# Weight slots split and released in halves of the contraction

## The chip, the core and the metric

The kernel runs on one core of one Trainium2 chip. The metric is the time of one execution on the device in microseconds (us). Five engines with queues of their own take part: PE (TensorE, matmuls; PEld is its weight load), DVE (VectorE), ACT (ScalarE), POOL (GpSimd), and SP, which here issues the transfers of weights. They wait for each other through semaphores only, and each takes its instructions in the order of its program.

## The reference, cut to what matters

Two transformer-like blocks over 256 tokens of width 1024 in fp32. The first block has two layers that also carry a context stream of 256 tokens. All matrix products have the form below; norms, modulation and attention stand between them.

```python
def adaln_in(x, g, shift, scale):
    return rmsnorm(x, g) * (1 + scale) + shift

def adaln_out(x, y, g, gate, weight):
    return x + weight * gate * rmsnorm(y, g)

def swiglu(h, w_gu, w_down):
    gu = h @ w_gu
    return (jax.nn.silu(gu[..., :D_FF]) * gu[..., D_FF:]) @ w_down

def ffn_sublayer(x, mod, k, g_pre, g_post, w_gu, w_down):
    h = adaln_in(x, g_pre, mod[k], mod[k + 1])
    return adaln_out(x, swiglu(h, w_gu, w_down), g_post, mod[k + 2], HALF_STEP)
...
        merged = (jax.nn.sigmoid(gate_a[:, :s]) * (y_nsa @ w_up_nsa[i])
                  + jax.nn.sigmoid(gate_b[:, :s]) * (y_moba @ w_up_moba[i]))
        x = x + merged @ w_out[i]
```

## The kernel before, in words

All weights pass in 305 **units** (`weight_units`), at most 128 x 2048 numbers (1 MB): 8 chunks of the contraction (k) by 256 output columns for gate-up, projections and mixers, 10 or 12 chunks by 128 columns for the down projections (dn..a and dn..b). A unit is used for the 256 tokens of x (X), the 256 of the context (Z), or all 512. Some gate-up phases are split in ax (tokens of X) and az (of Z), some down phases in bx and bz, so that the norms of one stream run beside matmuls of the other.

Products are made in two parts: w = w_hi + w_lo and h = h_hi + h_lo, and for each k three matmuls are issued, (w_hi, h_hi), (w_hi, h_lo), (w_lo, h_hi) (`PARTS`). So each unit goes through four engines, with two slots (u % 2) of w_raw, w_hi and w_lo:

- SP (`sync_program`, L386): waits until w_lo of unit u-2 is made in both halves, then loads w_raw of unit u.
- ACT (`high_split`, L1260): waits for the transfer and for PE's end with unit u-2 (unit_done), and copies w_raw to w_hi in two halves of the slot.
- DVE (`low_split`, L802): subtracts, w_lo = w_raw - w_hi, in the same halves. These are the halves of the contraction, since k is the outer index of the slot.
- PE (`feature_unit`, L454; `token_unit`; `up_phase`): waits for both halves of w_lo and for the evacuation of unit u-2, and runs all its matmuls: for each 128 output columns m, all k.

ACT and DVE follow an order written out by hand: `turn_of(u)` evacuates unit u from PSUM, splits unit u+2, and finishes u's result (for gate-up: hid and its low part). In a `window`, each turn is followed by `beside(code)`, a few steps of a norm: "v" and "V" are a root (rows named tok), "0" to "3" add a pair of chunks of the residual and square it, "a" to "d" make a pair of chunks of h and its low part. POOL adds the squares (ssum). PE runs the sums over partitions (L436) and the spread of the root (L443) at fixed places between a unit's matmuls (`norms_at`). In some gate-up units DVE also makes the modulation vectors (`mod_products`, L784). `attention` runs between phases; the weights of two units are ready before it.

## Time and profile before

| | before |
|---|---|
| median of 3 runs | 2483.17 us (2473.91 to 2485.79) |
| the profiled execution | 2485.29 us |
| its span | 2483.6 us |
| PE busy | 2318.9 us (93%), 14514 matmuls |
| DVE busy | 1470.1 us (59%) |
| ACT busy | 1030.4 us (41%) |
| POOL busy | 121.1 us (5%) |
| mean granted TensorE clock | 0.933 |
| w_lo halves on DVE | 610, 659.1 us |
| w_hi halves on ACT | 610, 556.9 us |
| a 1 MB weight transfer, issue to landing | 4.8 us median |
| HBM traffic | 151 GB/s over the span |

The span runs from the first to the last instruction. A granted clock of 1.00 is 2.4 GHz, 0.50 is 1.2 GHz; a value between them is the mean over a stretch at the two levels. Matmuls overlap, so PE's busy time is not its rate; the count of matmuls in a stretch over its length is. "[2.05 <-DVE w_lo L807]" behind an instruction is the idle time of its engine just before it, and what ended it.

### The profile page before, as it was taken

What the parts mean: (1) busy time and instruction counts of PE and PEld (TensorE: products, weight loads), DVE (VectorE), ACT (ScalarE), POOL (GpSimd) and SP (SyncE); (2) the same over time, 40 slices, a digit from 0 to 9 for tenths busy, and PEclk for the clock granted to TensorE, in tenths of its full rate; (3) what the DMA queues carried; (4) which work ended last, traced back from release to release, by engine and by line L of the source; (5) the groups of instructions that cost most, each with busy time, mean ns of one, the idle gap of its engine ahead of it and who ended that gap; (6) DMA issues with size and microseconds to landing.
All of it is one profiled execution on the core that took longest, in us unless ns stands there. A gap on an engine that the chain in (4) does not pass through costs nothing. (4 is left out here: it accounts for less than half of the span.)

```text
span 2483.6 us, 35308 instructions
## 1 busy us (share of the span) xinstructions
PE 2318.9 (93%) x14514; PEld 2026.6 (82%) x14514; DVE 1470.1 (59%) x2453; ACT 1030.4 (41%) x1729; POOL 121.1 (5%) x83
## 2 busy tenths in 40 slices
PE   5999998999899999899999988969997999999998
PEld 2988888898798888889888886569997875588998
DVE  5675775667566677565677565635554544345555
ACT  3422224643652223563222354544444544334443
POOL 1000001100200000100000020010000010000000
PEclk8999999999999999999999998979998995589999
DMA  6545554455345555445555442015555420024553
GB/s 255 196 158 200 187 166 156 138 202 169 119 170 168 199 179 171 149 147 174 185 190 178 157 166 89 1 51 172 202 178 195 153 87 16 1 102 147 181 175 127
DMA packets 70362, 376.08 MB, mean 151 GB/s; under 512 B 7454, under 2 KB 12190, under 8 KB 43834
## 3 DMA queue, kind: packets, MB, share of 16 engines
q1 hardware_dynamic: 67536, 367.81, 43.5%
q10 hardware_dynamic: 2666, 6.02, 0.7%
q8 instruction: 115, 1.88, 0.3%
q14 instruction: 45, 0.37, 0.0%
HBM read 372.75 MB, written 1.05 MB: 151 GB/s over the span
## 5 line engine op out<-in xcount | busy, mean ns | idle before, releaser
L467 PE MATMUL ps_g<-h,w_hi 128*128 128x256 f32 (+1 forms) x4224 | 999.3, 331 | 19.1 <-DVE h L874 10.3
L807 DVE TENSOR_TENSOR w_lo<-w_raw,w_hi 128x1024 fp32r<-128x1024 f32 (+2 forms) x610 | 659.1, 1122 | 321.8 <-ACT w_hi L1267 321.4
L467 PEld LDWEIGHTS ps_g<-h,w_hi 128*128 128x128 f32 x4224 | 719.0, 192 | 99.1 <-DVE w_lo L807 11.2
L467 PE MATMUL ps_g<-h,w_lo 128*128 128x256 f32 (+1 forms) x2112 | 695.7, 329 | 0.0
L1267 ACT ACTIVATE w_hi<-w_raw 128x1024 fp32r<-128x1024 f32 (+2 forms) x610 | 556.9, 963 | 204.1 <-PE ps_g L467 180.2
L467 PE MATMUL ps_g<-hid,w_hi 128*128 128x256 f32 (+1 forms) x2368 | 501.2, 310 | 18.9 <-DVE w_lo L807 15.3
L467 PEld LDWEIGHTS ps_g<-h,w_lo 128*128 128x128 f32 x2112 | 405.2, 192 | 36.8
L467 PEld LDWEIGHTS ps_g<-hid,w_hi 128*128 128x128 f32 x2368 | 389.0, 193 | 44.4 <-DVE w_lo L807 17.4
L467 PE MATMUL ps_g<-hid,w_lo 128*128 128x256 f32 (+1 forms) x1184 | 364.6, 308 | 0.0
L1366 ACT ACTIVATE gate_tmp<-ps_g 128x256 f32<-128x256 f32 (+1 forms) x144 | 65.2, 453 | 628.8 <-PE ps_g L467 628.8
L467 PE MATMUL ps_g<-b_h,w_hi 128*128 128x256 f32 x1504 | 282.6, 291 | 10.5 <-DVE b_h L874 7.3
L467 PEld LDWEIGHTS ps_g<-b_h,w_hi 128*128 128x128 f32 x1504 | 240.3, 196 | 14.4 <-issue 9.6
L911 DVE TENSOR_TENSOR prod<-gate_tmp,ps_g 128x256 f32<-128x256 f32 (+1 forms) x128 | 66.6, 521 | 302.3 <-ACT gate_tmp L1366 302.3
L467 PEld LDWEIGHTS ps_g<-hid,w_lo 128*128 128x128 f32 x1184 | 228.3, 193 | 11.0
L467 PE MATMUL ps_g<-b_h,w_lo 128*128 128x256 f32 x752 | 216.8, 288 | 0.0
L1604 POOL TENSOR_TENSOR ssum<-ssum,sq 128x512 f32<-128x512 f32 x72 | 110.4, 1534 | 2161.5 <-ACT sq L1275 2161.5
L784 DVE CUSTOM_DVE_ANT_0 ps_s<-mod_raw,cond_b,vecs 128x1024 f32<-128x1024 f32 x128 | 164.9, 1289 | 0.5 <-DMA mod_raw<-in_w_mod 0.5
L784 DVE CUSTOM_DVE_ANT_0 mod_raw<-mod_raw,cond_b,vecs 128x1024 f32<-128x1024 f32 x128 | 164.0, 1281 | 0.0
L467 PEld LDWEIGHTS ps_g<-b_h,w_lo 128*128 128x128 f32 x752 | 147.6, 196 | 0.0
L436 PE MATMUL ps_s<-mats,ssum 128*128 128x1 f32 x192 | 29.8, 277 | 53.4 <-POOL ssum L1604 53.4
L436 PEld LDWEIGHTS ps_s<-mats,ssum 128*128 128x128 f32 x192 | 28.2, 226 | 57.3 <-POOL ssum L1604 57.3
L1370 ACT ACTIVATE y<-ps_g 128x512 f32<-128x512 f32 (+1 forms) x32 | 17.4, 544 | 134.9 <-PE ps_g L467 134.9
(237 smaller groups left out, 1890.1 us busy)
## 6 DMA issues: line engine op xcount, KB each, us to landing
w_raw<-in_gu SPq DMA_DIRECT2D x128, 1024.0 KB, 4.8
mod_raw<-in_w_mod SPq DMA_DIRECT2D x128, 512.0 KB, 3.6
w_raw<-in_conv_cu SPq DMA_DIRECT2D x16, 1024.0 KB, 4.9
w_raw<-in_dn00b SPq DMA_DIRECT2D x16, 768.0 KB, 4.2
w_raw<-in_dn01b SPq DMA_DIRECT2D x16, 768.0 KB, 4.2
w_raw<-in_dn10b SPq DMA_DIRECT2D x16, 768.0 KB, 4.3
w_raw<-in_conv_out SPq DMA_DIRECT2D x8, 1024.0 KB, 4.8
w_raw<-in_w_in_a SPq DMA_DIRECT2D x8, 1024.0 KB, 4.8
```

The source lines that it names most:

```text
L436: mm = pe.matmul(ps_s[:, s, S + j:S + j + 1], pair_of(ssum, s)[:, a, j * P:(j + 1) * P], ones[:, 0:1], start=(a == 0), stop=(a == 1))
L467: mm = pe.matmul(ps_g[:, 2 * (u % 2) + m, cs], w[wp][:, k, m * P:(m + 1) * P], acts[ap][:, k, cs], start=(k == 0 and n == 0), stop=(k == k ...
L784: dve.tensor_tensor_reduce(dump if s == 0 else w, w, cond_b[:, s, :], 1.0, b_mod[:, g, s:s + 1], ALU.mult, ALU.add, mod_sb[:, g, s:s + 1]) ...
L807: dve.tensor_tensor(w_lo[u % 2][:, cols], w_raw[u % 2][:, cols], w_hi[u % 2][:, cols].bitcast(F32), ALU.subtract).then_inc(lo_made, 1)
L911: dve.tensor_tensor(prod[:, j, cs], gate_tmp[:, j, cs], ps_g[:, 2 * j + 1, cs], ALU.mult).then_inc(evac, 1)
L1267: act.activation(w_hi[u % 2][:, cols], w_raw[u % 2][:, cols], ACT.Copy).then_inc(hi_made, 1)
L1366: act.activation(gate_tmp[:, j, cs], ps_g[:, 2 * j, cs], ACT.Silu if ph[:2] == "gu" else ACT.Copy).then_inc(gate_made, 1)
L1370: act.activation(y[:, ul, cs], ps_g[:, 2 * j, cs], ACT.Copy).then_inc(evac, 1)
L1604: pool.tensor_tensor(ssum[:, s, :], ssum[:, s, :], sq[:, s, :], ALU.add).then_inc(sq_added[s], 1)
```

## The change

A new semaphore half_done tells that PE has read the first half of a unit's contraction for the last time. PE runs a unit as two halves: first k 0 to 3 (for 8 chunks) for all m, then the rest for all m, and waits for each half's w_lo apart. ACT and DVE split by half: `turn_of(u)` makes only the second half of unit u+2, and after it (and, in windows on DVE, after the norm steps) `high_ahead(u)` and `low_ahead(u)` make the first half of unit u+3, which ACT starts when unit u+1 is half done. Where unit u+3 is larger than unit u+1 (`grows`), that half waits for the whole unit, and in windows ACT takes it behind the norm steps; elsewhere ACT takes it ahead of them. The sum over k has the same terms in the same order; the transfers are issued on the same condition.

```diff
@@ tensor_program, feature_unit @@
-            pe.wait_ge(lo_made, 2 * u + 2)
-            if u >= 2:
-                pe.wait_ge(evac, u - 1)
-            for m in range(mt):
-                for k in range(kc):
...
-            mm.then_inc(unit_done, 1)
+            for half in range(2):
+                pe.wait_ge(lo_made, 2 * u + half + 1)
+                if half == 0 and u >= 2:
+                    pe.wait_ge(evac, u - 1)
+                for m in range(mt):
+                    for k in range(half * kc // 2, (half + 1) * kc // 2):
...
+                mm.then_inc(half_done if half == 0 else unit_done, 1)
@@ token_unit @@
+                    if k == NC // 2 - 1 and (i + 1) * P == UNITS[u].cols.stop:
+                        mm.then_inc(half_done, 1)
@@ vector_program @@
-        def low_split(u):
-            half = UNITS[u].elems // 2
-            for n in range(2):
+        def low_half(u, n):
+            if u < len(UNITS):
+                half = UNITS[u].elems // 2
...
+        def low_split(u):
+            low_half(u, 0)
+            low_half(u, 1)
+        def low_ahead(u):
+            low_half(u + 3, 0)
+        def low_put_off(u):
+            low_half(u + 2, 1)
+            low_ahead(u)
@@ vector_program, turn_of @@
-            if not keep_off and u + 2 < len(UNITS):
-                low_split(u + 2)
+            if not keep_off:
+                low_half(u + 2, 1)
@@ vector_program, window @@
                 turn_of(u, hid)
                 beside(code, o, i, s, h1)
+                low_ahead(u)
@@ vector_program, up_phase @@
-                low_split(u + 2)
+                low_half(u + 2, 1)
                 dve.wait_ge(merge_hi, ul + 1)
                 dve.tensor_tensor(h2[1][:, 2 * ul:2 * ul + 2, :], merged,
                                   h2[0][:, 2 * ul:2 * ul + 2, :].bitcast(F32), ALU.subtract).then_inc(merge_lo, 1)
+                low_ahead(u)
@@ scalar_program @@
+        def high_half(u, n):
+            if u < len(UNITS):
+                half = UNITS[u].elems // 2
+                cols = slice(n * half, (n + 1) * half)
+                if n == 0:
+                    act.wait_ge(raw_in[u % 2], 16 * (u // 2 + 1))
+                if u >= 2:
+                    act.wait_ge(half_done if n == 0 and not grows(u) else unit_done, u - 1)
+                act.activation(w_hi[u % 2][:, cols], w_raw[u % 2][:, cols], ACT.Copy).then_inc(hi_made, 1)
+        def grows(u):
+            return UNITS[u].elems > UNITS[u - 2].elems
@@ scalar_program, window @@
                 turn_of(u, hid)
-                beside(code, o, i, s, h1)
+                if grows(u + 3):
+                    beside(code, o, i, s, h1)
+                    high_ahead(u)
+                else:
+                    high_ahead(u)
+                    beside(code, o, i, s, h1)
```

The same is done in `attn_layer`, `projections` and `up_phase` of each engine, where `low_ahead(u)` or `high_ahead(u)` stands behind `turn_of(u)` (in `attn_layer` on DVE ahead of the rotations), and behind `attention`.

DVE at the end of the first feed-forward layer's second gate-up phase, before the change (w_lo1 is the odd slot, L784 the products, L929 the add into y of the first dn0bx unit):

```order
L807 TENSOR_TENSOR w_lo1<-w_raw1,w_hi1 128x768 x2
L938 TENSOR_TENSOR hid1<-prod,hid0 128x512
L784 ISA ps_s,mod_sb<-mod_raw0,cond_b,vecs 128x1024
L784 ISA mod_sb 128x1
L784 ISA mod_raw0,mod_sb<-mod_raw0,cond_b,vecs 128x1024
L784 ISA mod_sb 128x1
L784 ISA ps_s,mod_sb<-mod_raw1,cond_b,vecs 128x1024
L784 ISA mod_sb 128x1
L784 ISA mod_raw1,mod_sb<-mod_raw1,cond_b,vecs 128x1024
L784 ISA mod_sb 128x1
L929 TENSOR_TENSOR y<-y,ps_g 128x256
L807 TENSOR_TENSOR w_lo0<-w_raw0,w_hi0 128x768 x2
```

The same place now (L811 is the split, L954 hid's low part, L788 the products, L945 the add into y):

```order
L811 TENSOR_TENSOR w_lo1<-w_raw1,w_hi1 128x768
L954 TENSOR_TENSOR hid1<-prod,hid0 128x512
L788 ISA ps_s,mod_sb<-mod_raw0,cond_b,vecs 128x1024
L788 ISA mod_sb 128x1
L788 ISA mod_raw0,mod_sb<-mod_raw0,cond_b,vecs 128x1024
L788 ISA mod_sb 128x1
L788 ISA ps_s,mod_sb<-mod_raw1,cond_b,vecs 128x1024
L788 ISA mod_sb 128x1
L788 ISA mod_raw1,mod_sb<-mod_raw1,cond_b,vecs 128x1024
L788 ISA mod_sb 128x1
L811 TENSOR_TENSOR w_lo0<-w_raw0,w_hi0 128x768
L945 TENSOR_TENSOR y<-y,ps_g 128x256
```

One half of the odd slot has moved ahead of this piece, and one half of the even slot stands ahead of the add into y; its second half follows that add.

ACT beside the first units of dn0bz, before (L1267 the split, L1308 the scaling by the gate, L1299 the root, L1275 squares):

```order
L1267 ACTIVATE w_hi0<-w_raw0 128x768 x2
L1308 ACTIVATE gate_tmp<-y,ab 128x256 x2
L1308 ACTIVATE prod<-y,ab 128x256 x2
L1299 ACT_TABLE_LOAD
L1299 ACTIVATE tok<-tok 128x2
L1267 ACTIVATE w_hi1<-w_raw1 128x768 x2
L1275 ACTIVATE ssum<-y 128x512
L1275 ACTIVATE ssum<-x 128x512
```

The same place now (L1302, L1359, L1350, L1326):

```order
L1302 ACTIVATE w_hi0<-w_raw0 128x768 x2
L1302 ACTIVATE w_hi1<-w_raw1 128x768
L1359 ACTIVATE gate_tmp<-y,ab 128x256 x2
L1359 ACTIVATE prod<-y,ab 128x256 x2
L1350 ACT_TABLE_LOAD
L1350 ACTIVATE tok<-tok 128x2
L1302 ACTIVATE w_hi1<-w_raw1 128x768
L1326 ACTIVATE ssum<-y 128x512
L1302 ACTIVATE w_hi0<-w_raw0 128x768
L1326 ACTIVATE ssum<-x 128x512
```

A half of the odd slot now stands ahead of the scalings, and a half of the even slot ahead of the squares of x.

DVE at the end of w_up, before (L1188 makes merged, L1191 its low part, L933 adds into x):

```order
L1188 TENSOR_TENSOR gate_tmp<-prod 128x512
L807 TENSOR_TENSOR w_lo1<-w_raw1,w_hi1 128x1024 x2
L1191 TENSOR_TENSOR b2_h1<-gate_tmp,b2_h0 128x512
L933 TENSOR_TENSOR x<-x,ps_g 128x2x256
L807 TENSOR_TENSOR w_lo0<-w_raw0,w_hi0 128x1024 x2
```

The same place now (L1219, L1222, L949):

```order
L1219 TENSOR_TENSOR gate_tmp<-prod 128x512
L811 TENSOR_TENSOR w_lo1<-w_raw1,w_hi1 128x1024
L1222 TENSOR_TENSOR b2_h1<-gate_tmp,b2_h0 128x512
L811 TENSOR_TENSOR w_lo0<-w_raw0,w_hi0 128x1024
L949 TENSOR_TENSOR x<-x,ps_g 128x2x256
```

One half now stands between merged and its low part instead of two.

## Rows read from the trace of the kernel before

**Rows 1.** Span and granted clock of the core.
```profile
core 0: 2483.6 us, clock 0.933
```

**Rows 2.** PE, PEld, DVE, ACT, POOL busy us (x), clock, DMA: 8 steady units.
```profile
2353.20:2398.80 45.60, 45.60 (x386) 45.60 (x385) 24.95 (x32) 20.66 (x32) 0.00 (x0) 1.00 0.52 179
```

**Rows 3.** PE's waits, us in total, times, longest.
```profile
PE ps_s L436 <- POOL ssum L1604: 53.4, 19, 10.2
PE ps_g L467 <- DVE w_lo L807: 24.4, 19, 2.6
PE ps_s L443 <- DVE tok L820: 20.3, 11, 5.5
...
PE ps_g L467 <- DVE h L874: 10.3, 8, 3.9
...
PE ps_g L549 <- DVE small L1171: 6.6, 1, 6.6
```

**Rows 4.** PE's matmul groups by shape: busy, mean ns, idle before, releasers.
```profile
L467 PE MATMUL ps_g<-h,w_hi 128*128 128x256 f32 x2560 | 477.9, 289 | 19.1 <-DVE h L874 10.3 <-DVE w_lo L807 8.7
...
L467 PE MATMUL ps_g<-hid,w_hi 128*128 128x256 f32 x1888 | 349.9, 288 | 18.9 <-DVE w_lo L807 15.3 <-DVE hid L950 2.6 <-DVE hid L1025 0.9
...
L467 PE MATMUL ps_g<-b_h,w_hi 128*128 128x256 f32 x1504 | 282.6, 291 | 10.5 <-DVE b_h L874 7.3 <-DVE b_h L1191 2.9 <-DVE w_lo L807 0.3
```

**Rows 5.** DVE in order of time from 359 (start, us).
```profile
359.43 1.83 DVE L807 TENSOR_TENSOR w_lo<-w_raw,w_hi 128x768 fp32r<-128x768 f32 x2
...
361.78 1.29 DVE L784 CUSTOM_DVE_ANT_0 ps_s<-mod_raw,cond_b,vecs 128x1024 f32<-128x1024 f32 x1
...
366.60 0.42 DVE L929 TENSOR_TENSOR y<-y,ps_g 128x256 f32<-128x256 f32 x1
366.93 1.82 DVE L807 TENSOR_TENSOR w_lo<-w_raw,w_hi 128x768 fp32r<-128x768 f32 x2
```

**Rows 6.** PE in order of time at 368.8 and 1668.6.
```profile
368.81 0.38 PE L467 MATMUL ps_g<-hid,w_hi 128*128 128x256 f32 x1 [2.05 <-DVE w_lo L807]
...
1668.56 0.55 PE L467 MATMUL ps_g<-h,w_hi 128*128 128x256 f32 x1 [3.39 <-DVE h L874]
```

**Rows 7.** Windows, second unit after the products, first two of three layers.
```profile
368.80:373.10 4.30, 4.29 (x36) 4.29 (x37) 2.02 (x3) 0.63 (x1) 0.00 (x0) 1.00 0.62 217
980.90:986.80 5.90, 5.86 (x36) 5.87 (x37) 2.05 (x3) 0.63 (x1) 0.00 (x0) 0.71 0.74 261
```

**Rows 8.** DVE and POOL in order of time from 416.
```profile
416.33 1.83 DVE L807 TENSOR_TENSOR w_lo<-w_raw,w_hi 128x768 fp32r<-128x768 f32 x2 [2.62 <-ACT w_hi L1267]
...
423.48 3.38 DVE L807 TENSOR_TENSOR w_lo<-w_raw,w_hi 128x768 fp32r<-128x768 f32 x2 [2.59 <-ACT w_hi L1267]
...
422.79 1.27 POOL L1604 TENSOR_TENSOR ssum<-ssum,sq 128x512 f32<-128x512 f32 x1 [0.80 <-ACT sq L1275]
```

**Rows 9.** ACT and PE in order of time from 401.
```profile
401.56 0.91 ACT L1308 ACTIVATE gate_tmp<-y,ab 128x256 f32<-128x256 f32 x2 [1.24 <-DVE ab L834]
...
405.04 1.22 PE L443 MATMUL ps_s<-mats,tok 128*128 128x128 f32 x4 [2.30 <-DVE tok L820]
```

**Rows 10.** PE's waits from 617 to 655.
```profile
PE ps_g L467 <- DVE w_lo L807: 5.0, 2, 2.6
```

**Rows 11.** Windows, the first two of three runs of norm windows.
```profile
394.30:712.30 318.00, 287.08 (x2115) 274.31 (x2114) 204.39 (x283) 168.98 (x270) 33.91 (x22) 0.96 0.45 154
1008.20:1115.30 107.10, 95.06 (x722) 92.96 (x721) 65.27 (x97) 65.61 (x108) 14.29 (x10) 0.92 0.41 143
```

**Rows 12.** DVE in order of time at 2212.
```profile
2211.99 2.35 DVE L807 TENSOR_TENSOR w_lo<-w_raw,w_hi 128x1024 fp32r<-128x1024 f32 x2
```

**Rows 13.** Windows, the first unit of w_out.
```profile
2209.80:2221.30 11.50, 8.60 (x51) 8.39 (x50) 4.85 (x6) 2.64 (x3) 0.00 (x0) 0.70 0.48 173
```

**Rows 14.** Windows, the second attention.
```profile
2043.00:2184.00 141.00, 132.74 (x397) 73.40 (x395) 58.22 (x337) 56.88 (x205) 2.45 (x2) 0.51 0.02 8
```

**Rows 15.** ACT's waits for a transfer of gate-up weights, whole span.
```profile
ACT w_hi L1267 <- DMA w_raw<-in_gu: 3.0, 2, 2.5
```

More of the change, by code:

```diff
@@ L723, in up_phase @@
                 w = [w_[u % 2][:].rearrange("p (k n) -> p k n", k=NC) for w_ in (w_hi, w_lo)]
-                pe.wait_ge(lo_made, 2 * u + 2)
-                pe.wait_ge(evac, u - 1)
-                for m in range(2):
-                    for src in range(2):
+                for src in range(2):
+                    pe.wait_ge(lo_made, 2 * u + src + 1)
+                    if src == 0:
+                        pe.wait_ge(evac, u - 1)
+                    for m in range(2):
                         for k in range(4):
@@ L732, in up_phase @@
                                                start=(k == 0 and n == 0), stop=(k == 3 and n == 2))
-                mm.then_inc(unit_done, 1)
+                    mm.then_inc(half_done if src == 0 else unit_done, 1)
         def ple():
@@ L957, in turns @@
                 turn_of(u, hid, last_off and u == us[-1])
+                if not (last_off and u == us[-1]):
+                    low_ahead(u)
         def window(us, codes, o, i, s, hid=None):
@@ L1155, in projections @@
             rotate2((0, 1), 1)
+            low_ahead(d[5])
             turn_of(d[6])
@@ L1254, in vector_program, with high_ahead, high_put_off @@
         between(None, 8, h2)
-        low_split(last_of("dn4b") + 2)
+        low_put_off(last_of("dn4b"))
         ple()
     def scalar_program():
-        def high_split(u):
-            half = UNITS[u].elems // 2
-            act.wait_ge(raw_in[u % 2], 16 * (u // 2 + 1))
-            if u >= 2:
-                act.wait_ge(unit_done, u - 1)
-            for n in range(2):
-                cols = slice(n * half, (n + 1) * half)
-                act.activation(w_hi[u % 2][:, cols], w_raw[u % 2][:, cols], ACT.Copy).then_inc(hi_made, 1)
+        def high_half(u, n):
[9 more added lines that the diff above has]
+            return UNITS[u].elems > UNITS[u - 2].elems
+        def high_split(u):
+            high_half(u, 0)
+            high_half(u, 1)
+        def high_ahead(u):
+            high_half(u + 3, 0)
+        def high_put_off(u):
+            high_half(u + 2, 1)
+            high_ahead(u)
         def squares(r, s, p, src):
@@ L1391, in turn_of @@
                                ACT.Copy).then_inc(evac, 1)
-            if not keep_off and u + 2 < len(UNITS):
-                high_split(u + 2)
+            if not keep_off:
+                high_half(u + 2, 1)
             if ph[:2] == "gu":
@@ L1420, in turns @@
                 turn_of(u, hid, last_off and u == us[-1])
+                if not (last_off and u == us[-1]):
+                    high_ahead(u)
         def window(us, codes, o, i, s, hid=None):
```

68 lines of the change are left out of this document (50 added, 18 removed).

## The prediction

> **What bounds the kernel now.** I read the span and clock first, then the table of who waits for whom on the matmul engine, then its matmul groups by shape, then single stretches in order of time. The profiled execution took 2485.29 us, of which 2483.6 are its span [rows 1]; 1.7 lie around it. The median of the runs shown is 2483.17, 2.1 below this execution, so the sum is made against 2485.3 and 2.1 come off at the end. PE is busy for 93% of the span. In a steady stretch it issues 384 weight matmuls of 8 units in 45.6 us, 119 ns each, at the full 2.4 GHz [rows 2]. That pace holds across the starts of the 8 units, where a wait on w_lo stands already; the change leaves it, since the matmuls are the same. So what can be won lies in PE's waits and in its clock.
>
> The waits [rows 3]: 53.4 us for the sums of squares, 24.4 for w_lo, 20.3 for the reciprocal root (tok), 6.6 for the last small rotation before the second attention. By shape [rows 4], w_lo holds up matmuls on hid for 15.3 us and on h for 8.7; in-phase waits for activations are 10.3 (h), 7.3 and 2.9 (b_h), 2.6 (hid L950). The change can reach the w_lo waits, some of the activation waits, and the work queued on DVE behind a low split.
>
> **1. The down phase after each gate-up phase.** DVE order after the last gate-up unit is: two low halves of the unit after next (1.83), the low part of hid, four products like the 1.29 shown, y's add, and only then the two halves that PE needs next (1.82 from 366.93) [rows 5]. PE restarts at 368.81 after 2.05 of waiting, so it had matmuls until 366.76 [rows 6]. There is one such place in each of the first three feed-forward layers, all of about the same length. The change takes one half (1.83/2 = 0.9) out of this run and puts the first needed half before y's add: it ends at 366.60 - 0.9 + 0.9 = 366.6, before PE asks at 366.76. The second half follows y's add, 366.6 + 0.33 + 0.9 = 367.8, and PE asks for it 18 matmuls later, at 368.9. Nothing is late next. Gain 3 x 2.03 = 6.1.
> After the first of the three waits the next unit ran at a granted clock of 1.00; after the second, and the third like it, at 0.71 for 5.9 us [rows 7]. So the same wait does not always cost clock; when it does, it costs (1 - 0.71) x 5.9 = 1.7. Bounds for the two: 0 and 3.4. I take 3.4, because nothing else idles PE there.
>
> **2. The windows in which norms run beside 256-column units.** What is left of w_lo after item 1 and item 4's 0.8 is 24.4 - 6.1 - 0.8 = 17.5, all in units beside which ACT and DVE do norms. The mechanism: ACT and DVE take a norm step whole between two splits. An example is unit 4 of the first dn0bz phase: w_lo's two halves start only at 416.33, because w_hi waited for ACT's norm work, and then again at 423.48 [rows 8]. Now the first half of a unit is split one unit earlier, and the second has until half the unit. So w_lo waits should go to nearly zero: +17.5. In-unit waits for h go too: 10.3 in 8 waits, of which the longest (3.9) and one of 3.4 stand before the first matmul of a phase and stay, so 3.0 go [rows 3, 6]: the first half now holds 24 matmuls instead of 12 before k = 4.
> Against it: PE then comes earlier to the sums and the spread, and these have their own chain. I walked the first dn0bz phase through. (a) ACT's four scalings start at 401.56, then comes the root; PE waits 2.30 for its result, until 405.04 [rows 9]. Now ACT first does a high half that waits for half of the unit PE is in (about 401.5), so the scalings start at 402.4: 0.85 later. (b) From then on every norm step on DVE starts one low half sooner after a unit's end. By the walk unit 4 starts 0.9 earlier than now although it began 0.85 late, its sums come 0.7 earlier, and the unit after it 2.0 earlier. Net 2.0 of the 2.6 that w_lo cost there. In the conv_out phase for ctx (5.0 us of w_lo waits [rows 10]) the same walk gives 3.5: unit 2 starts 2.7 earlier, but its sums only 1.2 earlier; then the spread, which has lost its DVE half, gives 1.5 back and the next norm step 0.8. Over all windows that is about 0.75 x (17.5 + 3.0) = 15. Bounds: 5 (only places without a sum behind them) and 24 (all w_lo waits, h, and 1 us off five of the sums).
> A low half takes 0.9 alone, but the two at 423.48 took 3.38 together while POOL added sums from 422.79, 1.27 us at a time [rows 8]. The Trainium skill (SBUF — State Buffer, section on the two separate sides) says that VectorE and GpSimd hold a shared port pair in turn, for a whole instruction. The row agrees: 3.38 - 1.83 = 1.55 were lost. By that rule, a half moved onto an add costs up to the add's 1.27, and one moved off gives it back; with 22 adds in 318 us [rows 11] and neither direction preferred I leave it at zero.
>
> **3. The clock in these windows.** It was 0.96 over 318 us, and 0.92 over 107.1 and over one more stretch like that [rows 11]: 0.04 x 318 + 0.08 x 214 = 29.8 us lost in all, some of it in gaps. Fewer waits can only help on average, but sums and tok, which stay, are the longer gaps there. I take 0; bounds -5 and +10.
>
> **4. Places where one low half stands before the value that PE needs.**
> Out projection of the second block: DVE has merged, then two low halves (2.35), then the low part b_h, for which PE waits 2.90 [rows 12]. One half goes behind b_h (1.15 sooner), and PE needs k = 6 after 30 matmuls instead of 18 (12 x 0.12 = 1.4 later). Gain 2.6. The clock was 0.70 in the 11.5 us of this unit [rows 13], (1 - 0.70) x 11.5 = 3.4, between 0 and 3.4; I take 2.5.
> First conv_out unit: the same with hid L950 (2.6 [rows 4]). One half less (1.15), 12 matmuls more before k = 6 (1.4): 2.3.
> Two phase changes from 10-chunk down to gate-up units where w_lo is 0.8 late in sum: 0.8.
> Before the second attention the chain on DVE is one half shorter (1.15 of 6.6): 1.0.
> Attention of the first block: DVE's rotations now stand behind a half that waits for the middle of a unit. Two of them are about 1 late each, while a sum comes 1.2 earlier: -1 to +1, taken as 0.
>
> **5. What the change adds.** One increment at half a unit, one more wait on PE per unit, about 140 more issue points on ACT and DVE; no new tile, no more bytes. A satisfied wait costs PE nothing at a unit's start: 119 ns there as elsewhere [rows 2]. The trace shows none in the middle of a unit; its bounds are 0 and one matmul lost per unit (0.12 x 300 = 36, slower), and the row nearest to it is the unit's start, so 0. In steady units of 5.7 us, ACT is busy 20.66 and DVE 24.95 of 45.6 us [rows 2], so the halves fit in either order, and a 1 MB transfer that lands in 4.8 now starts about 1.1 us sooner.
>
> **Sum.** 6.1 + 3.4 + 15 + 0 + 2.6 + 2.5 + 2.3 + 0.8 + 1.0 + 0 = 33.7. 2485.3 - 33.7 = 2451.6; less 2.1 gives 2449.5, forecast 2450.
>
> **Rivals.**
> A. The w_lo waits come back as waits for sums. For: 53.4 us of ssum waits stand in the same windows, and PE reaches each sum earlier. Then item 2 gives 3 and the clocks nothing: 6.1 + 3 + 6.7 = 16 less, 2467.
> B. The slots are limited by their transfers, and a release in halves changes nothing. For: 1 MB per 5.7 us is near what 4.8 us of landing allows, and transfers still start only when the whole unit's w_lo is done. Against: ACT's w_hi waits for a transfer of in_gu for 3.0 us in the whole span [rows 15], and the late w_lo of item 1 stood behind DVE's products. What is left then is b_h's earlier place: 2483 - 2.6 = 2480.
> C. Slower: the high half ahead stands in ACT's queue before the norm step and waits for half_done, so ACT idles while the norm chain that PE waits for stands behind it. Place: all chains of sums and tok beside 256-column units, some 14 of each. Its price is what I found for one of them, 0.85, up to the half unit of 2.1 to 2.9. It decides if the delay is over (33.7 + 12) / 28 = 1.6 us on each. With 2.1 on each it is 59 - 34 = +25, or 2508 at the median. Against: the walk found this delay once per window, with a gain of one DVE half after it. By the rule of the Trainium skill that ScalarE works strictly first in, first out (TensorE: Matmul & The Clock Gate, section on engine queue depths) the delay can't be avoided by the hardware; its size is what the rows give.
> D. The second attention runs at 0.51 of the clock for 141 us [rows 14]. If the shorter wait before it left it at full clock, up to 40 us more would go: 2410. Against: it did not recover in 130 us of busy PE, so the wait before it isn't what holds it down.
>
> **Chances.** Forecast 0.66 (2436 to 2461, which is item 3's +10 and half of item 2's span up to 24 on one side, 10 of item 2 on the other), A 0.17, B 0.08, C 0.05, D 0.04. The range takes in the forecast's bounds and A: 2434 to 2476. A measurement of this kernel tells 0.5% (12.4 us) from no change. Faster: 0.66 + 0.16 of A + 0.04 = 0.86; same 0.09; slower 0.05.
>
> **What would show it.** w_lo in PE's waits falls from 24.4 to under 4; the three 2 us waits in the down phases vanish and the units after them run at 1.00; b_h L1191 falls below 0.5; ssum plus tok stay within 5 us of their 73.7; steady units stay at 119 ns. Wrong if ssum and tok grow by more than 10 us (A or C), or if the steady pace changes.

## The result, and the profile after

The changed kernel took 2463.6 us (median of 4 runs, 2462.06 to 2468.3) against 2482.5 for the kernel before in the same comparison: ratio 0.993, 95% interval 0.9912 to 0.9948. That is about 18 us less. The forecast was 2450, in a range of 2434 to 2476. So the sign and the range hold, but 33.7 us were to go and about 18 did: 2463.6 lies above the forecast's own band (2436 to 2461) and is nearer to rival A's 2467. The profiled execution took 2462.86 us. Two executions at a far lower clock, one of the kernel before (7450.65 us) and one of e9_before_short (2820.21 us), stand outside every comparison and median here.

Span and clock of the changed kernel, for [rows 1]:

```profile
core 0: 2461.2 us, clock 0.935
```

PE's waits in the changed kernel (what was waited for and who made it, us in total, times, longest), for [rows 3]. The lines of before have moved: the sums are L436 <- L1678, the root tok L836, h L890, small L1202, the low part of hid L966, the rotation in the first attention layer L992, the add into y L945.

```profile
PE ps_s L436 <- POOL ssum L1678: 64.6, 19, 10.2
PE ps_s L443 <- DVE tok L836: 23.6, 12, 5.4
...
PE ps_g L468 <- DVE h L890: 8.4, 5, 3.9
PE ps_s L542 <- DVE y L992: 8.0, 3, 4.8
...
PE ps_g L552 <- DVE small L1202: 5.5, 1, 5.5
PE ps_g L552 <- DVE y L1078: 2.5, 1, 2.5
PE ps_g L468 <- DVE y L945: 2.0, 3, 0.7
...
PE ps_s L613 <- DVE gn L1151: 1.3, 1, 1.3
...
PE ps_g L468 <- DVE b_h L1222: 0.3, 1, 0.3
PE ps_g L468 <- DVE hid L966: 0.2, 1, 0.2
```

There is no line for w_lo left among the waits of PE's matmuls: 24.4 us before, none now. b_h before w_out went from 2.9 to 0.3 and hid from 2.6 to 0.2. But the sums grew by 11.2, tok by 3.3, the rotations from 4.1 to 8.0, and two waits are new (y L945, gn L1151).

Windows of the changed kernel (PE, PEld, DVE, ACT and POOL busy, clock, transfers): eight steady units, for [rows 2]; the second unit after the products in the first two layers, for [rows 7]; the first unit of w_out, for [rows 13]; the two runs of norm windows, for [rows 11], from and to the first matmul of the same units.

```profile
2328.78:2374.38 45.60, 45.60 (x387) 45.60 (x386) 25.40 (x32) 21.35 (x32) 0.00 (x0) 1.00 0.53 181
...
367.60:372.00 4.40, 4.36 (x37) 4.39 (x38) 2.83 (x4) 0.86 (x2) 0.00 (x0) 1.00 0.55 180
968.40:972.80 4.40, 4.34 (x36) 4.37 (x37) 2.85 (x4) 0.89 (x2) 0.00 (x0) 1.00 0.63 184
2191.30:2197.70 6.40, 6.06 (x52) 5.86 (x51) 4.94 (x6) 2.76 (x3) 0.00 (x0) 1.00 0.55 201
393.20:701.60 308.40, 288.60 (x2115) 276.86 (x2114) 203.97 (x281) 172.25 (x270) 36.79 (x22) 0.96 0.46 158
994.30:1094.80 100.50, 89.91 (x722) 88.36 (x721) 64.31 (x95) 66.07 (x108) 15.70 (x10) 0.97 0.43 149
```

The steady pace is what it was, 45.6 us for eight units. The second layer's unit ran at 1.00 instead of 0.71, and the first unit of w_out took 6.4 us at 1.00 where it took 11.5 at 0.70: 2.6 of the 5.1 us are the wait on b_h, the other 2.5 the clock. The two runs of norm windows fell from 318.0 to 308.4 us at the same clock, and from 107.1 to 100.5 us with the clock at 0.97 instead of 0.92.

Four places show where the rest went. First, the last units of the dn4b phase. ACT, DVE and PE of the changed kernel in order of time (start, us, what ran, idle before it):

```profile
2414.83 1.06 ACT L1302 ACTIVATE w_hi<-w_raw 128x1024 fp32r<-128x1024 f32 x1 [2.30 <-PE ps_g L468]
2415.92 1.23 DVE L811 TENSOR_TENSOR w_lo<-w_raw,w_hi 128x1024 fp32r<-128x1024 f32 x1 [1.61 <-ACT w_hi L1302]
2417.06 0.41 DVE L945 TENSOR_TENSOR x<-x,ps_g 128x256 f32<-128x256 f32 x1
2417.51 0.63 ACT L1326 ACTIVATE sq<-x 128x512 f32<-128x512 f32 x1 [1.62 <-DVE x L945]
2418.22 1.26 POOL L1678 TENSOR_TENSOR ssum<-ssum,sq 128x512 f32<-128x512 f32 x1 [9.09 <-ACT sq L1326]
2419.53 1.87 PE L436 MATMUL ps_s<-mats,ssum 128*128 128x1 f32 x8 [4.79 <-POOL ssum L1678]
```

The same stretch of the kernel before, in the same columns:

```profile
2439.25 0.42 DVE L929 TENSOR_TENSOR x<-x,ps_g 128x256 f32<-128x256 f32 x1 [0.80 <-PE ps_g L467]
2441.73 1.05 PE L436 MATMUL ps_s<-mats,ssum 128*128 128x1 f32 x8 [2.52 <-POOL ssum L1604]
```

The unit that is being split ahead (128x1024 a half) is larger than the one two before it (128x768), so its first half waits for the end of the unit that runs (`grows`). At that moment ACT's copy starts and DVE's subtraction stands behind it, and only then comes the evacuation of the unit that has just ended. So the last add into x starts 2.3 us later, and the square, POOL's add and the sums with it: 4.79 instead of 2.52. Units grow in this way at ten changes of phase, two at each (20 of the 305), and at five of the ten PE waits for a norm's sums. There the wait on the sums rose: at conv_cux (1.33 to 3.11), gu2ax (1.35 to 3.10), attn_kvx (1.33 to 2.75), dn3b's end (12.72 to 15.01) and here, 9.5 us in sum.

Second, DVE and PE beside the rotations of the first attention layer, in the changed kernel:

```profile
1486.50 1.22 DVE L811 TENSOR_TENSOR w_lo<-w_raw,w_hi 128x1024 fp32r<-128x1024 f32 x1
1487.63 0.69 DVE L991 TENSOR_TENSOR y<-q_raw,mod_raw 128x512 f32<-128x512 f32 x1
...
1489.07 2.05 PE L542 MATMUL ps_s<-q_raw,mats 128*128 128x512 f32 x2 [4.78 <-DVE y L992]
```

The half ahead stands directly in front of the rotation that PE waits for, in three places, 8.0 us together where one of 4.1 was before. (The next wait on the same chain, y L1078, fell from 5.4 to 2.5, so the net of it is 1.0 us.) These stages lost more than their waits. Their windows in the changed kernel, attn_kvx with attn_q and then attn_kvz with the first attention:

```profile
1433.20:1490.10 56.90, 46.24 (x320) 44.18 (x319) 32.95 (x44) 31.54 (x51) 6.19 (x4) 0.86 0.41 144
1490.10:1606.10 116.00, 109.02 (x550) 67.36 (x548) 62.72 (x216) 56.70 (x143) 0.00 (x0) 0.88 0.08 28
```

The same two windows of the kernel before:

```profile
1457.06:1509.60 52.54, 43.39 (x321) 41.03 (x319) 30.55 (x43) 31.42 (x51) 5.79 (x4) 0.92 0.45 156
1509.60:1621.93 112.33, 105.63 (x550) 66.07 (x548) 63.64 (x217) 56.38 (x143) 0.00 (x0) 0.90 0.09 29
```

They took 4.4 and 3.7 us less.

Third, ACT and PE in the first dn0bz phase, the place of [rows 9]:

```profile
400.56 0.84 ACT L1302 ACTIVATE w_hi<-w_raw 128x768 fp32r<-128x768 f32 x1 [2.22 <-PE ps_g L468]
401.31 0.89 ACT L1359 ACTIVATE gate_tmp<-y,ab 128x256 f32<-128x256 f32 x2
...
404.76 0.71 PE L443 MATMUL ps_s<-mats,tok 128*128 128x128 f32 x4 [3.25 <-DVE tok L836]
```

ACT idles 2.22 us for half a unit while the scalings, which need nothing of PE, stand behind that half. PE waits 3.25 instead of 2.30, in each of three layers.

Fourth, DVE at the place of [rows 5], after the products:

```profile
366.20 0.95 DVE L811 TENSOR_TENSOR w_lo<-w_raw,w_hi 128x768 fp32r<-128x768 f32 x1
367.07 0.41 DVE L945 TENSOR_TENSOR y<-y,ps_g 128x256 f32<-128x256 f32 x1
...
367.64 0.48 PE L468 MATMUL ps_g<-hid,w_hi 128*128 128x256 f32 x2 [0.69 <-DVE y L945]
```

w_lo is in time, but the evacuation behind it is not: 2.05 us of waiting became 0.69, and not 0.

### The profile page after: what moved, and what is told of

Read it like the earlier page. It is cut to its first block and busy times, and to the rows that moved or that the text cites. A ratio compares the mean times of both kernels' runs of the same rounds, so it can differ in the third digit from the quotient of the medians.

```text
span 2461.2 us, 35334 instructions
## 1 busy us (share of the span) xinstructions
PE 2309.7 (94%) x14514; PEld 2019.7 (82%) x14514; DVE 1480.6 (60%) x2453; ACT 1059.9 (43%) x1729; POOL 121.5 (5%) x83
## 3 DMA queue, kind: packets, MB, share of 16 engines
HBM read 372.75 MB, written 1.05 MB: 152 GB/s over the span
## 5 line engine op out<-in xcount | busy, mean ns | idle before, releaser
L811 DVE TENSOR_TENSOR w_lo<-w_raw,w_hi 128x1024 fp32r<-128x1024 f32 (+2 forms) x610 | 683.9, 1123 | 465.3 <-ACT w_hi L1302 464.6
L1302 ACT ACTIVATE w_hi<-w_raw 128x1024 fp32r<-128x1024 f32 (+2 forms) x610 | 588.3, 968 | 633.7 <-PE ps_g L468 526.0
L468 PE MATMUL ps_g<-hid,w_hi 128*128 128x256 f32 (+1 forms) x2368 | 495.1, 307 | 3.1 <-DVE y L945 2.0
L468 PE MATMUL ps_g<-b_h,w_hi 128*128 128x256 f32 x1504 | 275.9, 286 | 7.7 <-DVE b_h L890 7.3
L1678 POOL TENSOR_TENSOR ssum<-ssum,sq 128x512 f32<-128x512 f32 x72 | 111.4, 1549 | 2139.5 <-ACT sq L1326 2139.5
L1417 ACT ACTIVATE gate_tmp<-ps_g 128x256 f32<-128x256 f32 (+1 forms) x144 | 65.1, 452 | 331.2 <-PE ps_g L468 331.2
L788 DVE CUSTOM_DVE_ANT_0 ps_s<-mod_raw,cond_b,vecs 128x1024 f32<-128x1024 f32 x128 | 164.9, 1288 | 0.0
L788 DVE CUSTOM_DVE_ANT_0 mod_raw<-mod_raw,cond_b,vecs 128x1024 f32<-128x1024 f32 x128 | 164.0, 1281 | 0.0
L436 PE MATMUL ps_s<-mats,ssum 128*128 128x1 f32 x192 | 31.4, 285 | 64.6 <-POOL ssum L1678 64.6
L436 PEld LDWEIGHTS ps_s<-mats,ssum 128*128 128x128 f32 x192 | 29.8, 237 | 68.6 <-POOL ssum L1678 68.6
L468 PE MATMUL ps_g<-b_hid,w_hi 128*128 128x256 f32 x352 | 63.4, 283 | 0.0
```

The source lines that it names most:

```text
L436: mm = pe.matmul(ps_s[:, s, S + j:S + j + 1], pair_of(ssum, s)[:, a, j * P:(j + 1) * P], ones[:, 0:1], start=(a == 0), stop=(a == 1))
L468: mm = pe.matmul(ps_g[:, 2 * (u % 2) + m, cs], w[wp][:, k, m * P:(m + 1) * P], acts[ap][:, k, cs], start=(k == 0 and n == 0), stop=(k == k ...
L788: dve.tensor_tensor_reduce(dump if s == 0 else w, w, cond_b[:, s, :], 1.0, b_mod[:, g, s:s + 1], ALU.mult, ALU.add, mod_sb[:, g, s:s + 1]) ...
L811: dve.tensor_tensor(w_lo[u % 2][:, cols], w_raw[u % 2][:, cols], w_hi[u % 2][:, cols].bitcast(F32), ALU.subtract).then_inc(lo_made, 1)
L1302: act.activation(w_hi[u % 2][:, cols], w_raw[u % 2][:, cols], ACT.Copy).then_inc(hi_made, 1)
L1417: act.activation(gate_tmp[:, j, cs], ps_g[:, 2 * j, cs], ACT.Silu if ph[:2] == "gu" else ACT.Copy).then_inc(gate_made, 1)
```

## The experiments

Each kernel was timed beside the kernel before; the ratio to it is what is compared. The gain in us is (1 - ratio) x 2483; each interval is 2.5 us wide to either side for e7_split_only and 4 to 5 for the others, so two gains that differ by less than about 6 us aren't told apart by their times.

| kernel | ratio (95% interval) | gain, us | PE's waits: w_lo, sums, tok |
|---|---|---|---|
| the change | 0.9930 (0.9912 to 0.9948) | 17.4 | 0, 64.6, 23.6 |
| e1_grow | 0.9903 (0.9885 to 0.9921) | 24.1 | under 0.1, 56.9, 23.9 |
| e2_grow_rot | 0.9860 (0.9842 to 0.9878) | 34.8 | 0.1, 57.4, 23.0 |
| e3_pe_only | 0.9923 (0.9906 to 0.9939) | 19.1 | 8.0, 64.3, 18.1 |
| e4_norm_first | 0.9895 (0.9876 to 0.9915) | 26.1 | 0.7, 66.4, 17.0 |
| e5_all | 0.9814 (0.9798 to 0.9831) | 46.2 | 0.8, 59.1, 19.1 |
| e6_rot | 0.9892 (0.9876 to 0.9909) | 26.8 | 0.3, 65.1, 23.3 |
| e7_split_only | 1.0003 (0.9993 to 1.0014) | -0.7 | 24.2, 53.4, 19.2 |
| e8_ahead_only | 0.9947 (0.9932 to 0.9962) | 13.2 | 8.3, 60.5, 24.0 |
| e9_before_short | 0.9907 (0.9887 to 0.9927) | 23.1 | 26.3, 33.9, 22.2 |
| e10_pe_short | 0.9843 (0.9822 to 0.9864) | 39.0 | 6.9, 44.1, 23.8 |
| e11_all_short | 0.9753 (0.9732 to 0.9774) | 61.3 | 0.4, 43.1, 24.3 |

**e1_grow.** The first half of a growing unit is made in the turn, not ahead.

```diff
 def low_ahead(u):
-    low_half(u + 3, 0)
+    if not grows(u + 3):
+        low_half(u + 3, 0)
 def turn_of(u):
-    low_half(u + 2, 1)
+    if grows(u + 2):
+        low_half(u + 2, 0)
+    low_half(u + 2, 1)
```

(and the same with `high_half` on ACT)

> After the kernel's first unit of 1 MB, 2 MB behind a shorter one (a unit larger than the one two before it) has its first half made with its second half, in the turn, on ScalarE and VectorE; all else is the changed kernel. The theory: the five places where the changed kernel's sums wait grew (unit 50 of conv_cux 1.33 to 3.11 us, unit 131 of gu2ax 1.35 to 3.10, unit 184 of attn_kvx 1.33 to 2.75, the end of dn3b 12.72 to 15.01, the end of dn4b 2.52 to 4.79) are this half standing ahead of the evacuation behind which the sums wait. They sum to 9.5 us, and the wait on the sums falls from 64.6 to about 55 us; time 2451 to 2456, about 10 us under the changed kernel. The rival: the sums wait as long because they took over the waits on the low part (24.4 us before, none now), whatever stands ahead; then the wait on the sums stays within 2 us of 64.6 and the time within 3 us of 2463.6. A second rival: the half made in the turn is then late, and waits on the low part come back at those five places, 1.2 us each, and 6 us of the 10 are given back (2458).

Measured: 2459.7 us, and the sums wait 56.9. The waits at the ends of dn3b and dn4b are back at 12.71 and 2.51, exactly as before the change. At conv_cux and gu2ax half of it went (3.11 to 2.26, 3.10 to 2.13), at attn_kvx nothing (2.75): e5_all, which has the edits of e2 and e4 too, shows 1.98, 1.98 and 1.97 there, as much as e3_pe_only without any half in advance (1.93, 1.93, 1.92): the placements hold the rest down to there, and the last 0.6 us comes with PE's order. No wait on w_lo of over 0.1 us came back. The mechanism holds and both rivals fall, but the wait gave 7.7 us where about 10 were expected, and the time is 3.7 us above the upper end of what was expected. Its interval overlaps the changed kernel's, so the time by itself doesn't prove this step; the waits do.

**e2_grow_rot and e6_rot.** DVE's half ahead behind the rotations and behind the gate's low part (and ACT's behind the gate's high part), with e1's edit and without it.

```diff
 turn_of(u)
-low_ahead(u)
 rotate1(...)
+low_ahead(u)
```

> The kernel of the run e1_grow, and with it VectorE's first half of a unit ahead put behind the rotations in the first attention layer and behind the low part of the gate's norm at w_in (there on ScalarE too). The theory: the rotations' wait on TensorE (line 992 in the changed kernel, 8.0 us in 3 against 4.1 in 1 before) is due to the half that waits for half a unit ahead of them, so that 3 to 4 us of it go, and the 1.3 us on the gate's low part too: 4 to 5 us under the run e1_grow. The rival: the rotations stand in a chain of their own (turned on TensorE, three steps on VectorE each), so the order of one half changes nothing over 1 us.

> The changed kernel with the order in the first attention layer and at the gate's norm alone: VectorE's half ahead behind the rotations and behind the gate's low part, growing units as in the changed kernel. In the run e2_grow_rot this edit gave 12 us on top of e1_grow, where 4 to 5 were expected; by stage 3.6 us of them in attn_kvx and attn_q and 4.8 in attn_kvz and the first attention, 2.2 in w_in. The theory: the half ahead of the rotations is the whole loss of these stages, and the edit gives 8 to 11 us by itself: 2453 to 2456. The rival: it needs the growing unit 184 in its turn too (its half stands ahead of the squares of the same stage), and alone gives under 5 us: 2459 or more.

Measured: 2447.7 and 2457.2 us. In both the rotations wait 3.7 us once instead of 8.0 in three, and gn's 1.3 is gone; y L1078 is 4.3 instead of 2.5, so some 4 us of waits went. Against e1_grow the edit gives 10.7 us by the ratios, twice the expectation; against the changed kernel e6 gives 9.4 by the ratios, as its theory had it, and 6.4 by the medians, between the theory and the rival (2457.2 is 1.2 above the range of the theory). The windows of e6_rot for the two stages above:

```profile
1434.30:1490.80 56.50, 46.43 (x320) 44.22 (x319) 32.27 (x44) 32.10 (x52) 6.17 (x4) 0.87 0.41 145
1490.80:1600.90 110.10, 104.55 (x550) 65.17 (x548) 64.10 (x217) 56.61 (x143) 0.00 (x0) 0.92 0.08 29
```

The second stage is 5.9 us shorter than in the changed kernel, with 1.5 us fewer waits on PE and a clock of 0.92 instead of 0.88: most of it is clock. The first is as slow as in the changed kernel, and in e2_grow_rot it is level with before (52.2). There the growing unit 184 matters in its turn, as e6's rival said, but not for the whole.

**e4_norm_first.** ACT's norm step always ahead of its half ahead.

```diff
-if grows(u + 3):
-    beside(code, o, i, s, h1)
-    high_ahead(u)
-else:
-    high_ahead(u)
-    beside(code, o, i, s, h1)
+beside(code, o, i, s, h1)
+high_ahead(u)
```

> The changed kernel, but in the windows of the norms ScalarE always takes its norm step ahead of the high half of unit u+3 (in the changed kernel it takes it behind that half unless the unit grows). The theory: the half waits for half_done of the unit that runs, and a square or a root that stands behind it is late by up to half a unit; with the step ahead, the 0.95 us that the mean wait in the second stream's down phases grew (2.30 to 3.25, three of them) go, and so does part of the 4.4 and 2.4 us on the sums in gu1ax: 3 to 6 us under the changed kernel. The rival: the half behind a norm step comes late to VectorE, and waits on the low part come back: the windows have 15 us of them to lose, and the time goes 3 to 8 us above the changed kernel. Between them: no more than 2 us either way.

Measured: 2457.2 us, and tok 17.0 instead of 23.6. ACT and PE of this kernel at the place of [rows 9]:

```profile
400.30 0.91 ACT L1359 ACTIVATE gate_tmp<-y,ab 128x256 f32<-128x256 f32 x2 [1.11 <-DVE ab L850]
...
403.77 0.71 PE L443 MATMUL ps_s<-mats,tok 128*128 128x128 f32 x4 [1.40 <-DVE tok L836]
```

The time is 6.4 us lower by the medians and 8.7 by the ratios, a little more than the 3 to 6 expected. The wait is now 1.40, under the 2.30 of before the change: the edit takes away not only the 0.95 us that the change had added but 0.9 more in each of three places, since no half of unit u+3 and only one of unit u+2 now stands ahead of the norm step. The low part waits 0.7 us in one place: the feared return of 3 to 8 us did not come.

**e3_pe_only, e7_split_only, e8_ahead_only.** These take the change apart. e3 keeps PE's order half by half and its two waits, but makes both halves in the turn and waits for the whole unit; e7 takes PE's order back as well; e8 is the changed kernel with both waits at a unit's start.

```diff
# e3
 def low_ahead(u):
-    low_half(u + 3, 0)
+    return
...
-    low_half(u + 2, 1)
+    low_split(u + 2)
...
-act.wait_ge(half_done if n == 0 and not grows(u) else unit_done, u - 1)
+act.wait_ge(unit_done, u - 1)
# e7: e3, and PE's loops over m and k as before
# e8
-pe.wait_ge(lo_made, 2 * u + half + 1)
+pe.wait_ge(lo_made, 2 * u + 2)
```

> TensorE's order alone: a unit's matmuls run half by half with a wait on each half of the low part, and the splits are in halves, but both halves of unit u+2 are made in the turn of unit u (the first no earlier than before), and a weight slot is released whole, as before the change. The theory: the matmuls of the first half start one half of a low split earlier than before (2.45 us whole, 1.15 a half), so of each wait on the low part (24.4 us in 19) about 1.2 us go, the ones on h in the down phases (2.05 to 3.4 us before, together with them) shrink by about as much, and the small ones on hid and b_h (2.6 and 2.9) go whole; nothing of the five larger waits on the sums and nothing of the rotations comes, since no half stands ahead. Sum 10 to 16 us: 2468 to 2474. The rival: all the gain needs the half made in advance; then within 3 us of 2482.5. A second: the half-by-half order alone brings all of the gain or more (2464 or less), and making the half in advance earns nothing net.

> Of the change only the halved instructions: the high and the low split of a unit are two instructions each on ScalarE and VectorE, both in the turn, while TensorE waits for the whole low part and runs a unit in the order of before, and slots are released whole (at w_up and the token units as in the changed kernel). It is the run e3_pe_only without TensorE's order. The theory: halving costs and gains next to nothing (VectorE has about a fifth of its time free in the steady stretches and the second instruction begins right behind the first; the low half can begin when the high half is made, up to 1 us earlier than the whole), so 0 to 6 us under before (2478 to 2484), and TensorE's order holds the rest of the 20 us of e3_pe_only. The rival: the gain of e3_pe_only comes from the pipelining of high and low halves between ScalarE and VectorE, not from TensorE's order: 2466 or less.

> The changed kernel, but a feature unit's matmuls wait for both halves of the low part before the first; the order half by half, the release by halves and the half made in advance are as in the changed kernel. The theory: with one half made in advance only one is left in the turn, so that the waits on the low part shrink by a half's 1.2 us each much as in e3_pe_only; but the losses of the half ahead stay (8 to 11 us on the sums behind growing units, 8 at the rotations) and the waits on h in the down phases that the half order removes come back: 4 to 10 us under before, 2474 to 2480. The rival: with the half in advance TensorE's waiting by halves is worth nothing more: within 3 us of the changed kernel (2463.6).

Measured: 2463.1, 2482.2 and 2469.3 us. e7 came out as a control: the kernel before split each unit in halves already, so e7 differs from it only at the token units and w_up, where the half order stayed, and its waits and time are those of before. (The text on record for it speaks of the halving as a part of the change; it isn't. It also puts DVE's free time in the steady stretches at a fifth, where [rows 2] have 24.95 of 45.6 us busy.) Against e7 PE's order with its two waits gives 19.8 us (e3), as much as the whole change: e3's second rival was right, and its theory of 10 to 16 us fell short. The half in advance without the wait for each half gives 13.9 (e8, which keeps the order, since the release by halves needs it): 2469.3 lies between its theory (2474 to 2480) and its rival (within 3 us of 2463.6), and the waits on h (7.3) did not come back. Both together give 18.1. Their times barely tell the three apart. By their waits, the two means compete for the same waits on w_lo: of 24.4 us, e3 leaves 8.0 and e8 8.3. The losses at the rotations, at the ends of dn3b and dn4b and on tok come only with the half in advance: e3 has 4.0, 12.73, 2.51 and 2.35 us there, e8 8.1, 15.01, 4.79 and 3.23. PE's waits in e3_pe_only:

```profile
PE ps_s L436 <- POOL ssum L1676: 64.3, 19, 10.2
PE ps_s L443 <- DVE tok L836: 18.1, 10, 4.3
...
PE ps_g L468 <- DVE w_lo L811: 8.0, 8, 1.3
```

Here the sums wait 64.3 us too, and for another reason than in the changed kernel. The five growing places show 1.9, 1.9, 1.9, 12.7 and 2.5: the first three 0.6 up on before, the others not. What grew most are the units where a wait on w_lo stood before the sums (2.97 to 4.09 at conv_cux 4, 1.72 to 2.83 at conv_outz 2, 1.28 to 3.25 and 1.27 to 2.40 in gu1ax, 1.26 to 2.39 in gu2ax, 1.7 to 2.62 in three dn..bz): each grew by 0.9 to 2.0, 9.1 together, while w_lo gave up 0.6 to 1.7 there. That is rival A's mechanism, at work in eight places. In the changed kernel it shows at conv_outz 2 above all: the 2.61 us on w_lo went, and the sums went from 1.72 to 4.39.

**e9_before_short, e10_pe_short, e11_all_short.** The last of POOL's three adds of each sum takes 32 columns, so these kernels leave the other 480 columns of that pair of chunks out of the sum. e9 is built on the kernel before, e10 on e3, e11 on e5.

```diff
-pool.tensor_tensor(ssum[:, s, :], ssum[:, s, :], sq[:, s, :], ALU.add)
+n = 32 if p == 3 else T2
+pool.tensor_tensor(ssum[:, s, 0:n], ssum[:, s, 0:n], sq[:, s, 0:n], ALU.add)
```

> The kernel before the change, but the last of GpSimd's three adds of each sum of squares (24 sums) takes 32 columns instead of 512, which leaves the rest of that pair out of the sum: the chain behind which TensorE waits for the sums is shorter by about 1.2 us (an add takes 1.30). Rival A of the prediction said that waits on the low part come back as waits for the sums; in e3_pe_only the first fell by 16.4 us and the second grew by 10.9. If the two chains stand side by side (the norm's and the splits'), then here the sums wait loses up to 19 x 1.2 = 23 us, and where a wait on the low part follows directly (units 46, 54, 76, 78, 82, 127, 135, 180) that wait grows by what the sums gave, up to 8 x 1.2 = 10: the low part's waits go from 24.4 to 30 to 34 and the time falls by 13 to 19 us. The rival (the chains are apart, and the growth in e3_pe_only has another source): the low part's waits stay within 2 us of 24.4 and the time falls by 23 to 28.

> The kernel of the run e3_pe_only (TensorE's order alone) with the same shorter chain of sums as in e9_before_short (the last add of each sum takes 32 columns and leaves the rest out). If the chains stand side by side, the sums are what is late here, so the shorter chain gives its whole 1.2 us in nearly all 19 places: 22 to 28 us under e3_pe_only (2435 to 2441), which is 6 to 10 us more than it gives in e9_before_short; the order's gain, 19 to 20 us with the whole chain, is then 26 to 30. The rival: the two gains are equal within 3 us.

> The kernel of the run e5_all with the same shorter chain of sums. All waits on the low part are gone there (0.8 us) and the sums take 59.1 us of TensorE's waits in 19, so the chain of the norms is the only one left beside TensorE: the theory expects the whole 1.2 us of each, and the clock that goes with it, 22 to 28 us under e5_all, 2408 to 2414. The rival: ScalarE's and VectorE's halves ahead stand in the chain too, so that a shorter add only lets it wait for them: under 15 us.

Measured: 2459.0, 2441.6 and 2420.7 us. The shorter chain gave 23.1 us on the kernel before, 19.9 on e3 and 15.1 on e5, where 13 to 19, 22 to 28 and 22 to 28 were expected: the rivals were right on the first, and missed the other two by 0.2 us. The intervals of the three gains overlap, so the waits have to decide. The low part's waits in e9 rose by 2 us only, and at the eight units named in the expectation by 0.3 (12.97 to 13.30), where up to 10 were expected:

```profile
PE ps_s L436 <- POOL ssum L1605: 33.9, 18, 9.2
PE ps_g L467 <- DVE w_lo L807: 26.3, 20, 2.6
```

So the theory of two chains that take over from each other in both directions falls. The takeover has one direction: a wait on w_lo before the sums, once shortened, is in part waited again at the sums. A likely reason, which no run shows by itself, is that the norm's chain doesn't move with PE's order, while a shorter norm chain moves all that follows it, the splits too. The wait on tok rose in all three (20.3 to 22.2, 18.1 to 23.8, 19.1 to 24.3), so the halves ahead aren't what brings it. w_lo, sums and tok together fell by 15.7, 15.6 and 11.2 us, which is the order of the gains.

**e5_all.** e1, e2 and e4 in one.

> The kernels of the runs e2_grow_rot and e4_norm_first in one: growing units have both halves made in the turn, VectorE's half ahead stands behind the rotations and the gate's low part, and ScalarE's norm step always stands ahead of its half ahead. The theory: the two edits touch different places (e4's 6 us are mostly the wait on tok in the second stream's down phases, 3.25 to 1.4 us in three, and conv_outz and attn_kvx, where e2 changed little or gains the same 3 us), so they add up to 20 to 22 us under the changed kernel: about 4 to 6 us under the run e2_grow_rot, 2442 to 2444. The rival: both act on the same wait, the one of TensorE on the norm's sums, and what one gives the other can't; then it stays within 2 us of 2447.7.

Measured: 2436.3 us (2436.09 to 2439.3), ratio 0.9814: beyond the expectation of 2442 to 2444, and 27 us under the changed kernel. Its span and PE's waits:

```profile
core 0: 2437.6 us, clock 0.938
```

```profile
PE ps_s L439 <- POOL ssum L1685: 59.1, 19, 10.2
PE ps_s L446 <- DVE tok L845: 19.1, 13, 5.7
...
PE ps_s L545 <- DVE y L1001: 2.7, 1, 2.7
...
PE ps_g L471 <- DVE w_lo L814: 0.8, 1, 0.8
```

By single steps e1 gives 6.7, e6 9.4 and e4 8.7 over the changed kernel, 24.8 in sum; together 28.8. Within the intervals (4 to 5 us on each side of each) they add up. So where the half in advance stands in its queues decides what it is worth: with the change's placements nothing beyond PE's order, with these 27 us more. The 28.8 us are not all losses undone, since e4's edit and e2's bring waits below those of before.

## Why the prediction was right, and where its sum failed

By stage, from the first matmul of a stage to that of the next, in the profiled executions (us against the kernel before, minus is faster; the starts are those of the units' first matmuls in the traces). The last column is e7_split_only, whose waits are those of before: what it shows is how much single profiles differ by the clock alone.

| stages | predicted | after | e3_pe_only | e5_all | e7 |
|---|---|---|---|---|---|
| dn0bx, dn1bx, dn2bx (item 1) | -9.5 | -8.1 | -5.9 | -7.5 | -0.3 |
| dn..bz, conv_cu, conv_outz, gu1 and gu2 (item 2) | -15 | -13.5 | -4.6 | -20.4 | -3.9 |
| conv_outx | -2.3 | -2.7 | -1.6 | -2.7 | +1.1 |
| attn_kvx to the first attention | 0 | +8.1 | -0.2 | -4.1 | +0.3 |
| ends of dn3b and dn4b | 0 | +6.4 | +0.3 | +1.1 | +1.1 |
| w_out | -5.1 | -5.5 | -5.3 | -5.8 | -4.1 |
| all others | -1.8 | -7.1 | -7.0 | -6.6 | +2.0 |
| span | -33.7 | -22.4 | -24.3 | -46.0 | -3.9 |

- Item 1 held in its mechanism and nearly in its size. The 2.05 us waits on w_lo went and the clock of the second layer's unit came back to 1.00. The step "the first needed half before y's add" overlooked that y's add is itself what PE waits for: 0.69, three times, so the waits gave 4.1 us and not 6.1; the stages gave 8.1 with what the clock gave back.
- Item 2 was close, 13.5 of 15, though in part by luck: e7 shows 3.9 us less in these stages with the waits of before, and the reasons given aren't those that the runs show. The 0.85 us that the walk found for tok are there (0.95 measured), and e4 shows that they were avoidable. The "half a unit sooner" was put down to the half in advance; e3 shows that PE's order alone takes two thirds of the w_lo waits (16.4 us), and that the sums wait 10.9 us more.
- Item 4's w_out came as predicted in number, and conv_out too. The 2.6 us of the wait on b_h are the change's. The 2.5 of clock can't be put down to it: in e7_split_only the same wait of 2.9 us stands there, and the unit ran at 1.00 all the same.

```profile
2209.20:2218.10 8.90, 6.01 (x51) 5.80 (x50) 4.85 (x6) 2.64 (x3) 0.00 (x0) 1.00 0.62 226
```

- "Attention of the first block ... -1 to +1, taken as 0" is the first step that failed: +8.1. The prediction had named the cause (rotations behind a half that waits for the middle of a unit) and given it one us a time; PE's idle time in these stages grew by only 1.8 us; the other 6.3 went by at a lower clock, 0.86 and 0.88 for 0.92 and 0.90. So the mechanism was sized about right in waits, and what was missing is the clock lost beside them. That the two go together is shown by e2's edit, which moves only the half (+7.4 us in these stages in e1_grow, -1.0 in e2_grow_rot); that these gaps are what lowers the clock is argued. e2 and e5 bring the stages back to before or better.
- Item 5, "what the change adds" at 0, is the second: it priced the instructions and the satisfied waits on PE, but not the growing unit's half that stands ahead of an evacuation on DVE: 9.5 us of waits on the sums, 6.4 us of time at the ends of dn3b and dn4b alone. The front of this document quotes the condition (`grows`); no walk was made through a place where it is true. e1 shows it there.
- The prediction's own test fired: ssum plus tok rose from 73.7 to 88.2, by 14.5, more than the 10 at which it called itself wrong. Rival A's mechanism is real but the smaller part in the changed kernel, where most of the growth is the growing units' (e1 takes 7.7 of the 11.2 us away); rival C's mechanism (ACT held on half a unit ahead of a norm step) is real too, at 0.95 us in three places rather than 1.6 in 28, 2.9 us of waits in all, so it doesn't turn the sign; the 8.7 us of e4 are more than this loss. B fell (the low part's waits are gone), and so did D: the shorter wait before the second attention (5.5 for 6.6) left that stage as it was, about 1 us shorter.
- "All others" gave 5.3 us more than was forecast. It comes in e3 and e5 as well, though not in e7, and with hardly a wait in it: small pieces of clock. Item 3 had bounds of -5 and +10 for the clock, but in the windows of the norms only.
- So the total is a sum of errors of both signs: above all 14.5 us too slow in two places that stood at 0, and 5.3 too fast elsewhere. The range held because it took in rival A.

What stays open: how much of the 18 us is clock, and why the clock falls in one kernel and not in the next at the same place. Waits on PE fell by far less than the time in e3 (the lines that changed sum to some 13 us, the time to 19), and no run set the clock by itself. That the clock moves time with no change in the waits is shown: e7's profile is 3.9 us shorter than that of the kernel before.

## What to carry to other kernels

When work is made earlier to shorten a wait, look at what stands behind it in the same queue at the moment it waits: a half split in advance can cost as much as it brings if an evacuation, a rotation or a norm step that another engine needs is queued behind its semaphore. Put the early work last among what is ready, and treat the exceptions of the rule (here units that grow) as places of their own. And test the consumer's order alone first: reordering PE's matmuls, with a wait for each half, brought as much as the whole change with no work moved at all.
